# Up projections of two conv-FFN layers by seven block products instead of eight, with the gated hidden rows passed through DRAM

## The chip, the cores and the metric

One core of one Trainium2 chip runs the whole program in one launch. The metric is the device time of that launch in microseconds (us). The kernel before took 2473.97 us (median of 3 runs, 2472.31 to 2477.3).

## The reference, cut to what matters

The program is one inference step of a two-layer decoder trunk for 1024 prompt tokens and 8 requests of 8 tokens, 1088 tokens in all, width 1024. Layer 0 is a recurrent block and a gated conv-FFN; then shared keys and values are projected; layer 1 is sliding-window attention and a second conv-FFN. The change lies in the two conv-FFNs:

```python
D_FF = 3 * D_MODEL          # 3072
def conv_ffn(xn, buf, w_up, conv_w, conv_b, w_down):
    u = xn @ w_up                        # (1088, 1024) @ (1024, 6144)
    g, v = u[..., :D_FF], u[..., D_FF:]
    gc, new_buf = causal_dwconv(g, buf, conv_w, conv_b)   # width 3, along the tokens
    return (jax.nn.gelu(gc) * v) @ w_down, new_buf
```

`xn` is the RMS-normed residual stream. The kernel folds the norm's gain into the input of the product and multiplies by the per-token factor `rstd` behind it.

## The kernel before, in words

Channels lie on the 128 partitions and tokens along the free axis. `x` holds the residual stream as 8 rows (128 channels x 1088 tokens each). Every product keeps fp32 accuracy with three matmuls of a rounded type: an operand is split into a high part (ACT copies it into the rounded type) and a low part (DVE subtracts the high one), and weight-high x data-high, weight-high x data-low and weight-low x data-high are summed in PSUM (lines 886 to 888, function `piece`).

The unit of the order is a weight tile of 1024 x 128: SP loads it into `raw[s]` (slot s is 0 or 1, line 625), ACT makes `whi[s]` (`prep`, line 1426), DVE makes `wlo[s]` (`prep`, line 1977), and PE runs it against the 1088 tokens as three pieces of 384, 384 and 320 tokens, into three of six PSUM banks (slot 0: banks 0 to 2, slot 1: banks 3 to 5). A piece is 8 channel rows x 3 terms = 24 matmuls.

An FFN layer has 24 pairs of up tiles: slot 0 gives 128 channels of g, slot 1 the same channels of v. It goes in 4 blocks of 6 such pairs, and behind each block come 4 pairs of down tiles, which take the block's 6 rows of hidden values from SBUF and add into `x` (`residual`, line 2237). For each up pair DVE rescales g into `convin` (line 2315), runs the width-3 convolution (`conv`, lines 2093 and 2095), ACT takes the GELU (line 1730), DVE multiplies by `rstd` (2337) and by v (2341), and the hidden row is split into `sa` or `sb` (1734, 2348). POOL only copies the convolution's history and new state (2648, 2748, 2749).

Ahead of each FFN stand the 4 pairs of products of the block before it (`N_OUT`, or `N_O` in layer 1). While they run, ACT squares the finished rows of `x` (1649), POOL adds the squares (`add`, 2609), ACT and DVE split the rows (1665, 2263; the last two rows by pieces: 1676, 2274), and PE, ACT and DVE turn the sums into `rstd` (`stats` 916, `root` 1441, `recip` 1994). The split rows wait in SBUF as the input of all 48 up tiles.

The order is written out by hand: each engine has its own in-order program, counting semaphores join them, and the waits stand ahead of the instruction that needs them. SP issues all weight loads in the order of use.

Of the kernel before, what the change touches and what calls it, by code (L numbers as in the profile page):

```python
# [20 lines left out]
P = 128  # L21
# [9 lines left out]
DEC_B = 8  # L31
# [29 lines left out]
N_KV = N_F0 + NFB * (FB + KD // 2)  # L61
# [3 lines left out]
N_END = N_F1 + NFB * (FB + KD // 2)  # L65
# [38 lines left out]
def build(nc, A):  # L104
    with ExitStack() as ctx:
# [23 lines left out]
        reg_end = top[0]  # L129
        raw = [take(f"raw{s}", [P, KD * P], F32) for s in range(2)]  # L130
        whi = [take(f"whi{s}", [P, KD * P], F32R) for s in range(2)]
        wlo = [take(f"wlo{s}", [P, KD * P], F32R) for s in range(2)]
        convin = take("convin", [P, 1120], F32)
        y = take("y", [P, T], F32)
# [64 lines left out]
        def spare(j):  # L199
# [4 lines left out]
                   [spare(11 + k) for k in range(4)] + [spare(j) for j in (1, 3, 5, 15)])  # L204
        fout = at("fout", [18, D_FF], F32, reg_a)
# [48 lines left out]
        hhi_done = sem("hhi_done")  # L254
        hlo_done = sem("hlo_done")
# [63 lines left out]
        x_dram = nc.dram_tensor("x_spill", [P * KD * T], F32, kind="Internal").ap().rearrange("(p k t) -> p k t", p=P, k=KD)  # L319
        strip_in_sb = at("strip_in_sb", [BUCKETS + 1, FV + HEADS], F32, reg_v)  # L320
# [62 lines left out]
        def roots_base(v):  # L383
            return 3 * (v - 1)
# [4 lines left out]
        def xs_tiles(p):  # L389

            return 12 * p
# [196 lines left out]
        def _(eng):  # L588
# [113 lines left out]

            def ffn(layer, n0):
                up, down = A["f_w_up"][layer], A["f_w_down"][layer]
                with eng.Fori(0, NFB) as b:
                    with eng.Fori(0, FB) as j:
                        for s in range(2):
                            load(n0 + b * (FB + KD // 2) + j, s, w_cols(up, s * D_FF + b * (FB * P) + j * P), KD * P)
                    with eng.Fori(0, KD // 2) as i:
                        for s in range(2):  # L710
                            src = down.rearrange("(k p) n -> p k n", p=P)[:, ds(b * FB, FB), ds(i * 256 + s * P, P)]
                            load(n0 + b * (FB + KD // 2) + FB + i, s, src, FB * P)

            ffn(0, N_F0)
# [93 lines left out]
            out_weights(range(2, KD))  # L808
            ffn(1, N_F1)
# [35 lines left out]
        def _(pe):  # L845
# [65 lines left out]
            def stats(v, c):  # L911

                pe.wait_ge(sq_added, sq_base(v) + 22 + c)
                if c == 2:
                    pe.wait_ge(stat_sqrt, roots_base(v) + 1)
                pe.matmul(bank(6 + c % 2, c), ones[:, :], t2[:, chunk(c)], start=True, stop=True).then_inc(stat_ready, 1)  # L916
# [172 lines left out]
            def ffn(layer, n0, m, h, p, v):  # L1089
                hidden_split = ([h[:, k, :] for k in range(FB)], [h[:, FB + k, :] for k in range(FB)])  # L1090

                def block_(b, first, last):
                    nb = n0 + b * (FB + KD // 2)
                    f1 = layer * FT + b * FB + FB
                    if first:
                        unit(nb, 0, KD, m, split_done(p, v))
                        unit(nb, 1, KD, m)
                    with pe.Fori(1 if first else 0, FB) as j:
                        unit(nb + j, 0, KD, m)
                        unit(nb + j, 1, KD, m)  # L1100

                    def hidden(c, k):
                        if c == 0 and k == 0:
                            pe.wait_ge(hlo_done, 3 * f1 - 3)
                        if k == FB - 1:
                            pe.wait_ge(hlo_done, 3 * f1 - 2 + c)
                    if last and layer == 1:
                        for i in range(KD // 2):
                            for s in range(2):
                                pe.wait_ge(hi_ready[s], nb + FB + i + 1)  # L1110
                                pe.wait_ge(lo_ready[s], nb + FB + i + 1)
# [1712 lines left out]
```

## Time and profile before

| | |
|---|---|
| time, median of 3 | 2473.97 us |
| span of the profiled execution | 2473.6 us |
| TensorE (PE) busy | 2461.9 us, 15299 matmuls |
| VectorE (DVE) busy | 1235.0 us |
| ScalarE (ACT) busy | 775.1 us |
| GpSimd (POOL) busy | 270.4 us |
| granted TensorE clock, mean | 0.997 |

The profile is of one execution, whose span is within 0.4 us of the median. PEld is TensorE's loading of weights, which overlaps its matmuls. A matmul's row gives its whole passage, so neighbours overlap; how fast they follow each other is read from their starts. A releaser is what ended an engine's idle time.

### The profile page before, as it was taken

To read this page: it belongs to the slowest core of one execution; us is meant where nothing else is said; L and a number is where in the kernel's file an instruction comes from. 1 tells how busy PE (TensorE), PEld (TensorE's weight loads), DVE (VectorE), ACT (ScalarE), POOL (GpSimd) and SP (SyncE) were. 2 spreads that over 40 slices of the span, in tenths; PEclk is the share of its full clock that TensorE was granted. 3 is DMA by queue.
4 is the path that set the end of the run, shared out by engine and by line. 5 is a ranking of instruction groups with operands and counts; after the bars stand their busy time and mean duration, and the time that the engine had idled before them with its cause. 6 is when DMAs were issued, how large, how long until landed. Compare 5 with 4: busy or idle time off the path is not lost.

```text
span 2473.6 us, 39892 instructions
## 1 busy us (share of the span) xinstructions
PE 2461.9 (100%) x15299; PEld 2407.7 (97%) x15299; DVE 1235.0 (50%) x2008; ACT 775.1 (31%) x1272; POOL 270.4 (11%) x390
## 2 busy tenths in 40 slices
PE   9999999999999999999999999999999999999999
PEld 8999999999999999999999868999999999999999
DVE  7666645434443553444467675455335425434442
ACT  6554633212211321112344684332113113211221
POOL 4212520000000000001220353200000000000000
PEclk9999999999999999999999999999999999999999
DMA  4111111111111111111373203111111111111112
GB/s 127 44 51 43 52 43 43 38 47 51 42 38 47 49 38 49 43 44 37 120 114 72 70 1 107 43 49 40 38 51 42 41 53 42 38 47 51 42 36 92
DMA packets 227190, 130.96 MB, mean 53 GB/s; under 512 B 24789, under 2 KB 224669, under 8 KB 226876
## 3 DMA queue, kind: packets, MB, share of 16 engines
q1 hardware_dynamic: 224948, 126.47, 17.5%
q10 hardware_dynamic: 2100, 3.37, 1.2%
q8 instruction: 53, 0.87, 0.2%
q14 instruction: 25, 0.20, 0.0%
q0 software_dynamic: 64, 0.05, 0.0%
HBM read 116.76 MB, written 15.01 MB: 53 GB/s over the span
## 4 chain that ended last, share of the span: by engine, by line
PE 97%; DVE 1%; ACT 1%; DMA 0%; issue 0%; POOL 0%; POOLq 0%; DVEq 0%; ACTq 0%
PE ps L886 30%; PE ps L888 30%; PE ps L887 30%; PE ps L1264 1%; PE ps L1292 1%; PE ps L1316 1%; PE ps L1187 0%; PE ps L1364 0%; PE ps L1180 0%; PE ps L1365 0%; PE ps L1366 0%; PE ps L1085 0%; PE ps L1066 0%; PE ps L916 0%; PE ps L1198 0%
## 5 line engine op out<-in xcount | busy, mean ns | idle before, releaser
L886 PE MATMUL ps<-sa,whi 128*128 128x384 f32 (+1 forms) x1836 | 600.2, 327 | 0.1
L888 PE MATMUL ps<-sa,wlo 128*128 128x384 f32 (+1 forms) x1836 | 599.1, 326 | 0.0
L887 PE MATMUL ps<-sa,whi 128*128 128x384 f32 (+1 forms) x1836 | 598.6, 326 | 0.0
L886 PE MATMUL ps<-sb,whi 128*128 128x384 f32 (+1 forms) x1764 | 581.8, 330 | 0.0
L888 PE MATMUL ps<-sb,wlo 128*128 128x384 f32 (+1 forms) x1764 | 575.7, 326 | 0.0
L887 PE MATMUL ps<-sb,whi 128*128 128x384 f32 (+1 forms) x1764 | 575.2, 326 | 0.0
L1426 ACT ACTIVATE whi<-raw 128x1024 fp32r<-128x1024 f32 (+1 forms) x201 | 198.3, 986 | 867.1 <-PE ps L888 852.0
L886 PEld LDWEIGHTS ps<-sa,whi 128*128 128x128 f32 x1836 | 344.6, 188 | 1.4 <-issue 0.7
L887 PEld LDWEIGHTS ps<-sa,whi 128*128 128x128 f32 x1836 | 344.6, 188 | 0.3
L888 PEld LDWEIGHTS ps<-sa,wlo 128*128 128x128 f32 x1836 | 344.6, 188 | 0.0
L886 PEld LDWEIGHTS ps<-sb,whi 128*128 128x128 f32 x1764 | 331.3, 188 | 2.8 <-issue 1.2
L887 PEld LDWEIGHTS ps<-sb,whi 128*128 128x128 f32 x1764 | 331.3, 188 | 1.4
L888 PEld LDWEIGHTS ps<-sb,wlo 128*128 128x128 f32 x1764 | 331.1, 188 | 0.0
L1977 DVE TENSOR_TENSOR wlo<-raw,whi 128x1024 fp32r<-128x1024 f32 (+1 forms) x203 | 237.5, 1170 | 149.7 <-ACT whi L1426 149.6
L2237 DVE TENSOR_TENSOR x<-ps,x 128x384 f32 (+3 forms) x216 | 115.0, 534 | 373.8 <-PE ps L888 373.8
L886 PE MATMUL ps<-sc,whi 128*128 128x384 f32 (+1 forms) x816 | 266.8, 327 | 0.2 <-POOL sc L2616 0.2
L888 PE MATMUL ps<-sc,wlo 128*128 128x384 f32 (+1 forms) x816 | 265.9, 326 | 0.0
L887 PE MATMUL ps<-sc,whi 128*128 128x384 f32 (+1 forms) x816 | 265.8, 326 | 0.0
L2315 DVE TENSOR_TENSOR convin<-ps,rstd 128x384 f32<-128x384 f32 x144 | 73.2, 510 | 213.7 <-PE ps L888 212.2
L2748 POOL COPY fstash<-convin 128x2 f32 x48 | 8.9, 184 | 1509.6 <-DVE y L2095 1509.6
L886 PEld LDWEIGHTS ps<-sc,whi 128*128 128x128 f32 x816 | 153.2, 188 | 1.2 <-POOL sc L2616 0.7
L887 PEld LDWEIGHTS ps<-sc,whi 128*128 128x128 f32 x816 | 153.2, 188 | 0.1
(369 smaller groups left out, 2564.1 us busy)
## 6 DMA issues: line engine op xcount, KB each, us to landing
raw<-in_f_w_up SPq DMA_DIRECT2D x96, 512.0 KB, 3.8
raw<-in_f_w_down SPq DMA_DIRECT2D x64, 384.0 KB, 3.4
raw<-in_a_w_in SPq DMA_DIRECT2D x16, 512.0 KB, 3.9
x_spill<-x SPq DMA_DIRECT2D x1, 4352.0 KB, 16.1
x<-x_spill SPq DMA_DIRECT2D x8, 544.0 KB, 5.6
xrows<-in_x_prompt SPq DMA_DIRECT2D x8, 512.0 KB, 7.0
raw<-in_a_w_out SPq DMA_DIRECT2D x8, 512.0 KB, 3.8
raw<-in_w_q SPq DMA_DIRECT2D x16, 256.0 KB, 3.8
```

The source lines that it names most:

```text
L886: pe.matmul(out, whi[s][:, w], mhi[k][:, chunk(c)], start=(k == 0), stop=False)
L887: pe.matmul(out, whi[s][:, w], mlo[k][:, chunk(c)], start=False, stop=False)
L888: last = pe.matmul(out, wlo[s][:, w], mhi[k][:, chunk(c)], start=False, stop=(k == nk - 1))
L1264: last[e] = pe.matmul(out, qz[h0:h0 + HD, 4 * a + j, b * WIN:(b + 1) * WIN], kf[h0:h0 + HD, a, key:key + 256 - k0], start=True, stop=True)
L1292: last = pe.transpose(ps[:, bk, j * P:(j + 1) * P], pb[i % NPB][:, j, h * P:(h + 1) * P], ident[:, :])
L1316: last = pe.matmul(ps[h0:h0 + HD, 6, :], v, pt_buffer(2 * p + e)[h], start=(h == 0 or b == 0), stop=(h == 1))
L1426: act.activation(whi[s][:, 0:cols], raw[s][:, 0:cols], ACT.Copy).then_inc(hi_ready[s], 1)
L1977: dve.tensor_tensor(wlo[s][:, 0:cols], raw[s][:, 0:cols], whi[s][:, 0:cols].bitcast(F32), ALU.subtract)\
L2237: ins = dve.tensor_tensor(xt, bank(b, c), xt, ALU.add)
L2315: dve.tensor_tensor(gp[:, FFN_W - 1 + lo:FFN_W - 1 + lo + w], ps[:, c, 0:w], rstd[:, lo:lo + w], ALU.mult)\
L2748: pool.tensor_copy(fstash[:, ds(f, 1), 0:2], gp[:, SEQ:SEQ + 2].rearrange("p (o w) -> p o w", o=1))
```

## The change

For each of the 24 units (128 channels of g and the same of v), the 1024 input channels are split into even and odd rows, the tokens into two halves of 544, and the outputs into g and v. The 2 x 2 x 2 block product, 8 block products before, is made by 7 with sums and differences of the weight blocks and of the data blocks (Strassen's scheme in Winograd's form). A block product is 4 rows x 3 terms x 2 pieces of 272 tokens = 24 matmuls, 168 in a unit. The seven data blocks (`combos`) are made once in a layer, around the start of its first unit, the sums of the weight blocks in every unit by POOL, and the results are combined from PSUM by ACT, DVE and POOL. All 24 units of a layer now run behind each other and the 16 rounds of down products behind them; a hidden row goes to DRAM when it is made and comes back when its down block needs it. `x` goes to DRAM ahead of the up products, since its place in SBUF is used, and comes back behind them. The down products themselves are as before. In the diff, behind `product` and the entry's `save` and `scale`, stand one unit's order on ACT, one unit's order on DVE, the part of DVE's entry that follows the last residual add, and one unit's order on POOL. A `weight_hi(layer, u, j)` or `weight_lo` is 512 columns of the weight block of product j.

```diff
+HT = T // 2
+HC = HT // 2
...
+        PRODUCTS = [("a", "B11", 0), ("b", "T1", 1), ("c", "B21", 0), ("a", "B22", 1), ("b", "T2", 2), ("c", "T3", 3),
+                    ("d", "T4", 2)]
...
+            def unit_load(layer, u):
+                gu, par = unit_no(layer, u), u % 2
+                if u == 0:
+                    for s in range(2):
+                        eng.wait_ge(lo_ready[s], (N_F0, N_F1)[layer])
+                elif u == 1:
+                    eng.wait_ge(c_lo, combo_at(layer, "T4", "all"))
+                else:
+                    eng.wait_ge(w_lo, NP * (gu - 1))
+                    eng.wait_ge(s_made, 4 * (gu - 1))
+                for s in range(2):
+                    src = w_cols(A["f_w_up"][layer], s * D_FF + u * P).rearrange("p (i e) n -> p i e n", e=2)
+                    for e in range(2):
+                        eng.dma_start(rawu[par][:, s, e, :, :], src[:, :, e, :]).then_inc(unit_raw[par], 16)
...
+            def product(layer, gu, j, before=None):
+                slot, name, g = PRODUCTS[j]
+                pe.wait_ge(w_lo, weights_at(gu, j))
+                if j in (2, 3):
+                    pe.wait_ge(p_copied, 2 * gu + j - 1)
+                elif j == 6:
+                    pe.wait_ge(u2_made, gu + 1)
+                else:
+                    wait(pe, {0: c11_out, 1: c12_made, 4: c21_made, 5: u3_made}[j], gu)
+                hi, lo = SLOT[slot][:, 0, :, :], SLOT[slot][:, 1, :, :]
+                tile = combos[layer][name]
+                more = j in (2, 3)
+                for i in range(4):
+                    for term in range(3):
+                        w = (hi, hi, lo)[term][:, i, :]
+                        for cc in range(2):
+                            if before and term == 0:
+                                before(cc, i)
+                            moving = tile[:, (0, 1, 0)[term], i, cc * HC:(cc + 1) * HC]
+                            last = pe.matmul(ps[:, 2 * g + cc, 0:HC], w, moving, start=(i == 0 and term == 0 and not more),
+                                             stop=(i == 3 and term == 2), skip_group_check=more)
+                last.then_inc(prod, 1)
...
+                def save(k):
+                    act.dma_start(f_dram[:, k, :], x[:, k, :]).then_inc(spilled, 16)
+                def scale(k):
+                    act.wait_ge(spilled, 16 * (KD * layer + k + 1))
+                    act.wait_ge(sq_done, sq_base(v) + 3 * k + 3)
+                    act.activation(x[:, k, :], x[:, k, :], ACT.Copy, scale=pcol[:, k, gain:gain + 1]).then_inc(scaled, 1)
...
+                for u in range(1, FT):
+                    weight_hi(layer, u, 2)
+                    weight_hi(layer, u, 6)
+                    product_copy(layer, u, 0)
+                    weight_hi(layer, u, 3)
+                    gelu(layer, u - 1)
+                    product_copy(layer, u, 1)
+                    weight_hi(layer, u, 4)
+                    weight_hi(layer, u, 5)
...
+                        weight_hi(layer, u + 1, 0)
+                        weight_hi(layer, u + 1, 1)
...
+                for u in range(1, FT):
+                    weight_lo(layer, u, 2)
+                    make_c21(layer, u - 1)
+                    weight_lo(layer, u, 6)
+                    weight_lo(layer, u, 3)
+                    scale_gelu(layer, u - 1)
+                    take_c11(layer, u)
+                    weight_lo(layer, u, 4)
+                    make_hidden(layer, u - 1)
+                    weight_lo(layer, u, 5)
...
+                        weight_lo(layer, u + 1, 0)
+                        make_u2(layer, u)
+                        make_c12(layer, u)
+                        make_u3(layer, u)
+                        weight_lo(layer, u + 1, 1)
+                    unit_conv(layer, u)
...
+                combo_lo(layer, "T2", "all")
+                combo_lo(layer, "T2", 3)
+                weight_lo(layer, 0, 4)
+                recip(v, 0)
+                recip(v, 1)
+                combo_lo(layer, "T3", "all")
+                combo_lo(layer, "T3", 3)
+                weight_lo(layer, 0, 5)
+                seq.settle()
+                take_c11(layer, 0)
+                combo_lo(layer, "T4", "all")
+                combo_lo(layer, "T4", 3)
+                weight_lo(layer, 0, 6)
+                recip(v, 2)
+                make_u2(layer, 0)
...
+                for u in range(1, FT):
+                    unit_state(layer, u - 1)
+                    unit_history(layer, u)
+                    weight_sum(layer, u, 3)
+                    if u < FT - 1:
+                        weight_sum(layer, u + 1, 0)
+                        weight_sum(layer, u + 1, 1)
+                    scale_c12(layer, u)
+                    make_c22(layer, u)
+                    if u < FT - 1:
+                        weight_sum(layer, u + 1, 2)
```

Beside these lines, the change moves the hidden rows: SP's `store(u)` writes a row when `make_hidden` is done, `stage(tt)` reads it back, and ACT's `hidden_hi` and DVE's `hidden_lo` split it, six rows in the last unit and one in each down tile from the second to the seventh of a block; SP's `back(k)` reads row k of `x` back behind the last unit. In the entry, `combo` (POOL, four subtractions of 544 columns for each of four row pairs), `combo_hi` (ACT) and `combo_lo` (DVE) make the split data blocks; the part "all" of a block is its first three rows, 1632 columns.

## Rows read from the trace of the kernel before

**Rows 1.** The page: busy time of the engines, and the chain that ended last.
```profile
PE 2461.9 (100%) x15299; PEld 2407.7 (97%) x15299; DVE 1235.0 (50%) x2008; ACT 775.1 (31%) x1272; POOL 270.4 (11%) x390
...
PE 97%; DVE 1%; ACT 1%; DMA 0%; issue 0%; POOL 0%; POOLq 0%; DVEq 0%; ACTq 0%
```
**Rows 2.** Busy time by engine in one window of up units; clock, DMA share.
```profile
1050.00:1100.00 50.00, 50.00 (x305) 50.00 (x304) 26.66 (x42) 10.54 (x14) 1.03 (x6) 1.00 0.14 42
```
**Rows 3.** Timeline of TensorE, in a piece of 320 and at pieces of 384.
```profile
1000.08 0.31 PE L887 MATMUL ps<-sa,whi 128*128 128x320 f32 x1
...
1001.54 0.31 PE L888 MATMUL ps<-sa,wlo 128*128 128x320 f32 x1
...
1004.84 0.33 PE L886 MATMUL ps<-sc,whi 128*128 128x384 f32 x1
...
1009.00 0.33 PE L886 MATMUL ps<-sc,whi 128*128 128x384 f32 x1
```
**Rows 4.** Instructions grouped by line and form: weight loads, and the cheap vector work.
```profile
L887 PEld LDWEIGHTS ps<-sa,whi 128*128 128x128 f32 x1836 | 344.6, 188 | 0.3
...
L1426 ACT ACTIVATE whi<-raw 128x1024 fp32r<-128x1024 f32 x137 | 144.3, 1053 | 496.8 <-PE ps L888 481.7 <-PE ps L1366 14.9 <-DMA raw<-in_a_w_in 0.2
...
L2337 DVE TENSOR_TENSOR y<-y,rstd 128x1088 f32<-128x1088 f32 x48 | 62.0, 1292 | 56.7 <-ACT y L1730 56.7
...
L1426 ACT ACTIVATE whi<-raw 128x768 fp32r<-128x768 f32 x64 | 54.0, 843 | 370.3 <-PE ps L888 370.3
L1730 ACT ACTIVATE y<-y 128x1088 f32<-128x1088 f32 x48 | 53.5, 1115 | 222.4 <-DVE y L2095 222.4
...
L2237 DVE TENSOR_TENSOR x<-ps,x 128x384 f32 x92 | 51.1, 556 | 149.1 <-PE ps L888 149.1
...
L1994 DVE RECIPROCAL rstd<-rstd 128x384 f32<-128x384 f32 x6 | 15.3, 2550 | 4.7 <-ACT rstd L1441 4.7
```
**Rows 5.** Timeline of DVE: splits of 512 and 1024 columns, and one convolution.
```profile
287.25 0.69 DVE L2250 TENSOR_TENSOR wlo<-raw,whi 128x512 fp32r<-128x512 f32 x1 [0.20 <-ACT whi L1658]
...
374.28 1.23 DVE L1977 TENSOR_TENSOR wlo<-raw,whi 128x1024 fp32r<-128x1024 f32 x1 [0.54 <-ACT whi L1426]
375.43 1.03 DVE L2093 TENSOR_SCALAR y<-convin,fcol 128x1024 f32<-128x1024 f32 x2
376.62 3.10 DVE L2095 SCALAR_TENSOR_TENSOR y<-convin,fcol,y 128x1024 f32<-128x1024 f32 x4 [0.16 <-DVE y L2093]
```
**Rows 6.** Timeline of POOL and DVE: POOL alone (twice), then both at once.
```profile
342.85 1.01 POOL L2609 TENSOR_TENSOR t<-t,t 128x384 f32<-128x384 f32 x1 [4.71 <-ACT t L1649]
...
96.69 2.54 POOL L2730 TENSOR_TENSOR z<-z 128x1088 f32<-128x1088 f32 x1
...
258.31 8.95 POOL L2699 TENSOR_TENSOR sa<-z,sa 128x320 fp32r<-128x320 f32 x6
...
264.74 1.78 DVE L1977 TENSOR_TENSOR wlo<-raw,whi 128x1024 fp32r<-128x1024 f32 x1
```
**Rows 7.** Transposes of 128 columns: six in the timeline; min/median/max ns of one.
```profile
2420.98 0.82 PE L1085 MATMUL ps<-ident,x 128*128 128x128 f32 x6
...
L1085 PE MATMUL ps<-ident,x x72: 270/272/300, 2414.6 to 2469.7; 128*128 128x128 f32 x64, 128*64 128x128 f32 x8
```
**Rows 8.** DMA issues, up weights: KB each and median us from issue to landing.
```profile
raw<-in_f_w_up SPq DMA_DIRECT2D x96, 512.0 KB, 3.8
```
**Rows 9.** Entry of layer 0: last residual add, sum behind the last squares, TensorE's pace.
```profile
361.69 0.48 DVE L2237 TENSOR_TENSOR x<-ps,x 128x320 f32<-128x320 f32 x1
...
353.02 1.01 POOL L2609 TENSOR_TENSOR t<-t,t 128x384 f32<-128x384 f32 x1 [3.35 <-ACT t L1649]
...
361.00:385.00 24.00, 24.00 (x145) 1.00 0.15 45
```
**Rows 10.** Attention: four-matmul groups of 32 columns, then the granted clock by windows.
```profile
1454.98 0.31 PE L1330 MATMUL ps<-pt,cv 128*64 128x32 f32 x4
...
1459.00:1462.00 3.00, 3.00 (x15) 2.24 (x15) 1.02 (x2) 2.24 (x9) 0.00 (x0) 0.50 0.01 3
```

More of the change, by code:

```diff
@@ new lines, in combo_part, with x_half, group, halved @@
+        def combo_part(layer, name, i, part):
+            tile = combos[layer][name]
+            return tile[:, part, 0:3, :] if i == "all" else tile[:, part, i, :]
+        def x_half(k, h):
+            return x[:, k, h * HT:(h + 1) * HT]
+        def group(g):
+            return ps[:, 2 * g:2 * g + 2, 0:HC]
+        def halved(ap):
+            return ap.rearrange("p (c t) -> p c t", c=2)
+        P1S, P5S, U2S, U3S = t1[:, 0:HT], t1[:, HT:T], t2[:, 0:HT], t2[:, HT:T]
+        C12S = y[:, 0:HT]
@@ L1087, in end_job @@
                 last.then_inc(tr_ready, 1)
[L1089 to L1100, printed above, removed]
-                    def hidden(c, k):
[L1103 to L1106, printed above, removed]
+            def product(layer, gu, j, before=None):
[5 more added lines that the diff above has]
+                    pe.wait_ge(u2_made, gu + 1)
+                else:
+                    wait(pe, {0: c11_out, 1: c12_made, 4: c21_made, 5: u3_made}[j], gu)
+                hi, lo = SLOT[slot][:, 0, :, :], SLOT[slot][:, 1, :, :]
+                tile = combos[layer][name]
+                more = j in (2, 3)
[9 more added lines that the diff above has]
+                last.then_inc(prod, 1)
@@ new lines, in ffn, with unit_pair, after_up @@
+            def ffn(layer, n0, v):
+                def unit_pair(h, first=False):
+                    for par in range(2):
+                        if first and par == 0:
+                            first_unit(layer, n0, v)
+                        else:
+                            for j in range(NP):
+                                product(layer, FT * layer + 2 * h + par, j)
+                unit_pair(0, True)
+                with pe.Fori(1, FT // 2 - 1) as h:
+                    unit_pair(h)
+                unit_pair(FT // 2 - 1)
+                for b in range(NFB):
+                    nb, last = n0 + b * (KD // 2), b == NFB - 1
+                    h = hidden_big(layer, b)
+                    hidden_split = ([h[:, k, :] for k in range(FB)], [h[:, FB + k, :] for k in range(FB)])
+                    def hidden(c, k):
+                        if c == 0:
+                            pe.wait_ge(h_lo, FT * layer + FB * b + k + 1)
+                    def after_up(s):
+                        if b == 0:
+                            done = FT * (layer + 1)
+                            for event in ((c11_out, c12_made), (c12_made, c21_made))[s]:
+                                pe.wait_ge(event, done)
@@ L1698, in state_copy @@
+            entry(0, N_OUT, "")
             def state_copy(layer, m):
@@ L1719, in ffn, with down_hi @@
             def ffn(layer, n0, phase):
[L1720 to L1741 removed]
+                def down_hi(s):
+                    act.wait_ge(prod, NP * unit_no(layer, FT - 1) + (4, 6)[s])
+                    prep(n0, s, FB * P, phase)
@@ L1742, in block_ @@
+                gelu(layer, FT - 1)
+                for b in range(NFB):
+                    nd, last = n0 + b * (KD // 2), b == NFB - 1
                     if last and layer == 0:
+                        act.wait_ge(c22_made, FT)
                         with act.Fori(0, KD // 2 - 1) as i:
@@ L2300, in end_copy @@
+            entry(0, N_OUT)
             def end_copy(m):
```

703 lines of the change are left out of this document (541 added, 162 removed).

## The prediction

> **What bounds the kernel now.** I read the page first: TensorE is busy for 2461.9 of 2473.6 us, and the chain that ended last is 97% TensorE [rows 1]. Nothing but its matmuls is worth removing. The windows say the same of the up units alone: 305 matmuls in 50 us, granted clock 1.00, DVE at work for 27 of 50 us, ACT for 11, POOL for 1 [rows 2]. So TensorE is full and the others have room, which is what the change spends. The page's 326 ns of a matmul is its passage, not its pace, so I take the pace from starts in the timeline: ten matmuls of 320 columns from 1000.08 to 1001.54, 146.0 ns each; 24 of 384 columns, the next piece's start included, from 1004.84 to 1009.00, 173.3 ns each [rows 3]. At clock 1.00, the 2.4 GHz level, the columns alone are 133.3 and 160.0 ns: each matmul costs its columns plus 13 ns. An up unit is 144 matmuls, 23.6 us by rows 2, and 48 of them are 1132.8 us.
>
> **The terms.** *Products.* A unit becomes 168 matmuls of 272 columns, 45,696 columns for 52,224: an eighth fewer, but 24 more matmuls. No row has 272 columns. From below, the columns alone are 113.3 ns; from above, the 320-column row, 146.0 ns. The line through the two rows of rows 3 gives 125.5, columns plus 13 ns gives 126.3; I take 126.0. It would fail if loading 128 columns of weights took longer. A load's row says 188 ns [rows 4], but it is a passage too: six transposes, each with its own 128-column load, pass in 0.82 us and one alone in 0.27, so they follow (0.82 - 0.27) / 5 = 0.11 us apart [rows 7]. That is below 126. A unit is then 168 x 0.126 = 21.2 us, 48 are 1016.1: **-116.7 us**.
>
> *Does the vector work keep up?* By columns: a 512-column split is 0.69 us on DVE [rows 5]; on ACT, (1053 - 843) / 256 = 0.82 ns a column gives 0.63 [rows 4]. A 544-column PSUM operation on DVE is 0.72 (556 ns at 384 columns, 1.05 a column from there to the 1292 of 1088 [rows 4]). The convolution is 1.03 + 0.16 + 3.10 = 4.3 [rows 5]. DVE in a unit: 7 x 0.69 + 5 x 0.72 + 4.3 + 2 x 1.29 = 15.3 us of 21.2. ACT: 7 x 0.63 + 2 x 0.6 + 1.1 = 6.8. POOL by rows 6, 1.01 at 384 and 2.54 at 1088 columns, 2.16 ns a column: four weight sums at 1.29, the scaling of the second half of g at 1.3, the fourth output block at 1.36, small copies 0.6: 8.4.
>
> Sums of busy time do not settle it; queues do. The narrowest loop: P5 ends; DVE makes u3 (0.72), splits the next unit's second weights (0.69), convolves (4.3), and only behind that, in its queue, splits the weights of product 2 of the next unit (0.69), for which TensorE waits. With 0.2 from the last matmul's step to its result (passage 0.33 less step 0.17 [rows 3], and a semaphore) that is 6.6 us. TensorE has P6, P0 and P1 to do meanwhile, 72 x 0.126 = 9.1, less 0.2 for the load. In just this stretch POOL makes the fourth block and a weight sum, 2.65 us. Both engines at once slow down: six 320-column subtractions on POOL took 8.95 us where 0.87 each would be 5.2, times 1.7, and DVE's 1024-column split 1.78 [rows 6] for 1.23 [rows 5], times 1.46. So POOL stretches to 4.5 us, DVE loses 4.5 x (1 - 1/1.46) = 1.4, and the loop is 8.0 of 8.9. It holds, by 0.9 us. The next narrowest, the split for product 4 behind `take_c11`, has 1.3 us in hand. The GELU no longer stands between products and down blocks: conv_done comes 1.9 us before ACT reaches it and the copy of P1 is needed 3 us after P1. I take **0** for stalls in the steady units, with 0 and 1.5 us a unit as ends.
>
> The Trainium skill, "GPSIMD Engine Reference", table of specifications, says that GpSimd's SBUF interfaces are shared with VectorE and contend where VectorE has two SBUF inputs. That rule speaks against this change, and rows 6 agree. Were the two fully exclusive, the loop would be 6.6 + 2.65 = 9.25 us of 8.9, 0.35 a unit, some 16 us in all.
>
> *Entry, twice.* Before, it cost nothing: behind the last add at 361.69, 145 matmuls follow in 24 us [rows 9]. Now, with E the end of the last out product:
> - The sum of squares of row 7's first piece is queued on POOL behind ACT, which waits for row 6's copy to DRAM: 4 us by the 512 KB row (3.8) [rows 8]. Before, POOL had it at 353.02 + 1.01, 7.6 us before E [rows 9]; now about 1.3 us after TensorE asks: 1.3.
> - P0 to P3 need only what is early; row 7 comes back scaled at E+7, and P3 ends near E+12.4. P4 needs DVE's part "all" of T2 (1632 columns, 1.9), T2's last row and weights: E+13.8. Then two reciprocals of 2.55 [rows 4] stand in DVE's queue before T3 (1.9 + 0.7) and its weights: P5 starts at E+21.9. P6 needs u2, which is behind c11, T4 (2.6), the weights and a third reciprocal of 320 columns (2.1): E+28.4. Unit 0 ends at E+31.5 instead of 21.2: 10.3.
> - Unit 1's raw weights lie in rows 4 and 5 of `x` and can't be loaded before T4's part "all" is split, E+24. One MB is 2 + 2 x 1.8 = 5.6 us (3.8 for half, of which I take 2 as fixed): E+30. On POOL two weight sums then stand before the scaling that unit 0's convolution needs, so it ends at about E+40, and product 2 of unit 1, due at 37.6, waits 3.1.
> Together 14.7, twice **+29.4 us**. Bounds: 5 (the 1.3 and one gap) and 25 each.
>
> *Clock.* In attention the granted clock fell to 0.50, the 1.2 GHz level, after sixteen groups of four 32-column matmuls, one of which is shown [rows 10]. The entry idles TensorE for 5 and 3.6 us with 3 us of work between. A fall would double P6's 3 us: I take **+6** for both entries; ends 0 and 15.
>
> *End of the up products, twice.* The last unit adds six splits of 1088 columns (1.29) and two of 768 on DVE, 8.4 us net, so 23.7 us for 21.2. But the first down tile asks for rows one at a time; row 5 is split at about +23.3, wanted at 21.2 + 2.6. c21 is ready at 28 to 30, wanted at 30.1. I take **+1** each, ends 0 and 5. Hidden rows (48 of 544 KB out and in) and `x` add some 70 MB to a DMA share of 0.14 [rows 2]; a row is 4 us and waited for in no unit. In the down blocks DVE has 1.65 + 0.96 + 1.29 = 3.9 us of 8.9 per tile (54 matmuls). Price 0; if a row came late, TensorE would wait its 4 us once a block.
>
> Sum: 2473.6 - 116.7 + 29.4 + 6 + 2 = 2394.7, and 0.4 for this execution against the median: **2395 us**.
>
> **The rivals.**
> - *DVE and POOL set the unit* (0.17). The loop above is 1 us longer than worked out, by harder contention or slower semaphores: 0.9 us of slack go, and each further us costs 46. For it: 0.9 us is little. Against: POOL is idle for 60% and the stretch was rated fully overlapped. At 1 us a unit: 2441.
> - *Slower, by weight loading* (0.09). Place: between any two of the 8064 matmuls. If the load can't keep up with 272 columns and the pace stays at the 320-column 146.0 ns, units are 24.5 us, 1177.3 in all: 2473.6 + 44.5 + 37.4 = 2556. It decides from (1132.8 - 37.4) / 8064 = 135.8 ns on. Against: 110 ns in rows 7, although those are plain fp32.
> - *Weights once for two pieces* (0.06). Both pieces now meet the same tile one after the other. The Trainium skill, "TensorE: Matmul & The Clock Gate", step-by-step part, says that weights may be loaded once and used by repeated matmuls. As a mechanism of this kernel: half of the 8064 matmuls would lose the 13 ns, -52 us: 2343. Against: lines 886 and 887 share weights already, and each has a load of its own, 1836 of them at 887 [rows 4], with no shorter step between them.
> - *No eighth less* (0.03): extra stalls of about 2.4 us a unit eat the gain and it comes out even.
>
> **How the numbers follow.** Likeliest (0.65): products at 124 to 129 ns and 15 to 50 us of stalls, 2370 to 2425. The range reaches up into the first rival: 2365 to 2450; outside are the weight-load case, part of the fast one and the worst loop. A measurement of this kernel can tell about 0.2%, 5 us. Faster 0.65 + 0.06 + 0.15 of the first rival = 0.86; within 0.2% 0.03; slower 0.09 + 0.02 = 0.11.
>
> **What would show it.** Starts of 272-column matmuls 126 ns apart; 21.2 us between the same product of two units; TensorE idle in units under 0.3 us; around each entry gaps before T2, T3 and T4 of 1.4, 5 and 3.5 us whose releasers are DVE's splits and u2; the first convolution waiting for POOL's scaling. A DVE release of product 2 in every unit means the first rival; a pace above 136 ns means the second.

## The result, and the profile after

The kernel after took 2395.67 us (median of 4 runs, 2395.09 to 2400.15) against 2473.88 us (4 runs, 2472.31 to 2477.3) for the one before: a ratio of 0.9684, 95% interval 0.967 to 0.9698, 78 us less. The forecast of 2395 us and its sign were right. The profiled execution is the longest of the four, 2400.15 us with a span of 2398.3, so against the span of before, 2473.6, the traces differ by 75.3 us.

The page of the kernel after, busy times and chain; it answers to [rows 1]:

```profile
PE 2350.5 (98%) x16451; PEld 2292.3 (96%) x16451; DVE 1545.9 (64%) x2120; ACT 873.6 (36%) x1486; POOL 823.8 (34%) x758
...
PE 89%; DVE 5%; issue 2%; POOL 1%; DMA 1%; ACT 1%; SPq 0%; POOLq 0%; DVEq 0%; ACTq 0%
```

TensorE has 1152 more matmuls and 111 us less work. DVE has 311 us more and POOL 553 us more; both were meant to be hidden. The chain is still mostly TensorE, but 5% of it is now DVE and 6% others, where it was 97% TensorE. Busy time by engine in two windows of up units (columns as in [rows 2]):

```profile
600.00:650.00 50.00, 50.00 (x402) 50.00 (x401) 39.96 (x49) 16.19 (x25) 25.22 (x25) 1.00 0.22 67
...
1750.00:1800.00 50.00, 50.00 (x401) 50.00 (x400) 38.53 (x48) 15.02 (x23) 26.92 (x25) 1.00 0.33 97
```

TensorE never waits there, at DVE's 40 of 50 us and POOL's 25 to 27. The count of a window takes in matmuls that lie across its edges, so the pace is read from starts. Timeline of TensorE, the last four products of unit 1 (start, duration, tile, shapes, count):

```profile
414.33 3.42 PE L1309 MATMUL ps<-b,slot_a 128*128 128x272 f32 x24
417.59 3.17 PE L1309 MATMUL ps<-t2c,slot_b 128*128 128x272 f32 x24
420.59 3.17 PE L1309 MATMUL ps<-t3c,slot_c 128*128 128x272 f32 x24
423.60 1.66 PE L1309 MATMUL ps<-t4c,slot_d 128*128 128x272 f32 x12
```

From 417.59 to 423.60 are 48 matmuls, 125.2 ns each (126.0 forecast). From unit to unit the same product starts 21.04 or 21.05 us apart in all 44 intervals behind unit 1 of either layer, without one exception. So the steady units have the time that TensorE needs and no more. What is lost lies at their two ends. The waits of TensorE over the whole program (waited for: us in total, times, longest):

```profile
PE ps L1309 <- DVE slot_c L2659: 12.6, 4, 3.5
PE ps L1309 <- DVE slot_b L2659: 6.5, 2, 3.3
PE ps L1309 <- issue: 3.8, 2, 2.0
PE ps L1116 <- POOL t L3078: 3.8, 3, 1.8
PE ps L1309 <- DVE slot_a L2659: 2.0, 2, 1.1
...
PE ps L1083 <- DVE sb L2723: 1.9, 1, 1.9
PE ps L1083 <- DVE sa L2723: 1.9, 1, 1.9
```

Those of up products (L1309) come twice in a layer at most. The timeline of TensorE at layer 0's entry shows where; [rows 9] had 145 matmuls in 24 us here:

```profile
357.74 0.91 PE L1116 MATMUL ps<-t,ones 128*128 128x384 f32 x2 [1.74 <-POOL t L3078]
363.06 3.16 PE L1309 MATMUL ps<-b,slot_a 128*128 128x272 f32 x24
...
374.03 3.17 PE L1309 MATMUL ps<-b,slot_a 128*128 128x272 f32 x24
380.42 4.76 PE L1309 MATMUL ps<-t2c,slot_b 128*128 128x272 f32 x24 [3.22 <-DVE slot_b L2659]
388.03 4.57 PE L1309 MATMUL ps<-t3c,slot_c 128*128 128x272 f32 x24 [2.85 <-DVE slot_c L2659]
394.57 3.23 PE L1309 MATMUL ps<-t4c,slot_d 128*128 128x272 f32 x24 [1.98 <-issue]
398.95 3.27 PE L1309 MATMUL ps<-b,slot_a 128*128 128x272 f32 x24 [1.15 <-DVE slot_a L2659]
...
408.72 5.81 PE L1309 MATMUL ps<-b,slot_c 128*128 128x272 f32 x24 [3.50 <-DVE slot_c L2659]
```

Read the durations too: a product of 24 matmuls passes in 3.17 us, and those behind the long gaps take 4.76, 4.57 and 5.81. There the granted clock has fallen towards the 1.2 GHz level: 0.71 in the window 381 to 389, against 0.98 in 373 to 381. DVE's splits of T2 and T3 in the same stretch, the first with POOL at work and the second with POOL idle:

```profile
374.83 4.72 DVE L2652 TENSOR_TENSOR t2c<-x,t2c 128x1632 fp32r<-128x1632 f32 x2
...
384.95 2.42 DVE L2652 TENSOR_TENSOR t3c<-x,t3c 128x1632 fp32r<-128x1632 f32 x2
```

**Where the 75 us come from.** A unit of the kernel before, 144 matmuls from start to start, in TensorE's timeline:

```profile
1060.99 0.34 PE L886 MATMUL ps<-sb,whi 128*128 128x384 f32 x1
...
1084.71 0.34 PE L886 MATMUL ps<-sb,whi 128*128 128x384 f32 x1
```

Up products: before, 23.72 us a unit (the steps of [rows 3] alone make 96 x 173.3 + 48 x 146.0 ns = 23.64); now 21.05; 48 x 2.67 = 128.2 us less. Entries, by starts: from unit 0's first product (363.06) to unit 1's last (423.60) are 60.54 us, where 13 products of 3.007 and the statistics' matmuls (0.65) would be 39.74; with the gap of 1.74 ahead, 22.5 us. Layer 1: 59.01 and 1.84, 21.1 us. Of these 43.6 us, 29.6 are idle, as the gaps' numbers add up (14.9 and 14.7); 14.0 are matmuls that follow more slowly: stretches at the lower clock, and the refilling of the pipeline behind each gap. Last product to first down tiles: 4.7 and 2.8 us over the matmuls' own time. -128.2 + 43.6 + 7.5 = -77.1, where the spans differ by 75.3. Of the 1.8 us between them 1.3 lie in attention, which the change does not touch: from its first to its last product of queries and keys are 95.5 us in this execution of the kernel before and 96.8 in this one of the kernel after. In the other traces that stretch is 94.0 to 96.8 us, so it is scatter.

### The profile page after: what moved, and what is told of

The parts are those of the page before. It is cut to its first block, busy times and chain, and to the rows that moved or that the text cites. A ratio compares the mean times of both kernels' runs of the same rounds, so it can differ in the third digit from the quotient of the medians.

```text
span 2398.3 us, 41262 instructions
## 1 busy us (share of the span) xinstructions
PE 2350.5 (98%) x16451; PEld 2292.3 (96%) x16451; DVE 1545.9 (64%) x2120; ACT 873.6 (36%) x1486; POOL 823.8 (34%) x758
## 4 chain that ended last, share of the span: by engine, by line
PE 89%; DVE 5%; issue 2%; POOL 1%; DMA 1%; ACT 1%; SPq 0%; POOLq 0%; DVEq 0%; ACTq 0%
PE ps L1309 38%; PE ps L1083 15%; PE ps L1085 14%; PE ps L1084 14%; PE ps L1520 1%; PE ps L1548 1%; PE ps L1572 1%; DVE y L2458 0%; PE ps L1443 0%; DMA stage<-h_spill 0%; DMA rawu<-in_f_w_up 0%; POOL t L3078 0%; DVE rstd L2359 0%; PE ps L1620 0%; PE ps L1436 0%
## 5 line engine op out<-in xcount | busy, mean ns | idle before, releaser
L1083 PE MATMUL ps<-sa,whi 128*128 128x384 f32 (+1 forms) x972 | 318.9, 328 | 2.4 <-DVE sa L2723 1.9
L1085 PE MATMUL ps<-sa,wlo 128*128 128x384 f32 (+1 forms) x972 | 317.6, 327 | 0.0
L1084 PE MATMUL ps<-sa,whi 128*128 128x384 f32 (+1 forms) x972 | 317.3, 326 | 0.0
L1309 PE MATMUL ps<-b,slot_a 128*128 128x272 f32 x2304 | 304.6, 288 | 2.0 <-DVE slot_a L2659 2.0
L1083 PE MATMUL ps<-sb,whi 128*128 128x384 f32 (+1 forms) x900 | 300.7, 334 | 2.6 <-DVE sb L2723 1.9
L1309 PEld LDWEIGHTS ps<-b,slot_a 128*128 128x128 f32 x2304 | 295.3, 189 | 2.5 <-DVE slot_a L2659 2.5
L1085 PE MATMUL ps<-sb,wlo 128*128 128x384 f32 (+1 forms) x900 | 294.7, 327 | 0.0
L1084 PE MATMUL ps<-sb,whi 128*128 128x384 f32 (+1 forms) x900 | 294.4, 327 | 0.0
L1083 PEld LDWEIGHTS ps<-sa,whi 128*128 128x128 f32 x972 | 182.8, 188 | 3.9 <-DVE sa L2723 2.2
L1084 PEld LDWEIGHTS ps<-sa,whi 128*128 128x128 f32 x972 | 182.8, 188 | 0.1
L3078 POOL TENSOR_TENSOR t<-t,t 128x384 f32<-128x384 f32 (+1 forms) x72 | 73.0, 1024 | 319.7 <-ACT t L1905 297.4
L1085 PEld LDWEIGHTS ps<-sa,wlo 128*128 128x128 f32 x972 | 182.7, 188 | 0.0
L1083 PEld LDWEIGHTS ps<-sb,whi 128*128 128x128 f32 x900 | 169.7, 189 | 5.7 <-DVE sb L2723 2.2
L1084 PEld LDWEIGHTS ps<-sb,whi 128*128 128x128 f32 x900 | 169.6, 188 | 1.1
L1085 PEld LDWEIGHTS ps<-sb,wlo 128*128 128x128 f32 x900 | 169.5, 188 | 0.0
L1309 PE MATMUL ps<-b,slot_c 128*128 128x272 f32 x1152 | 157.3, 294 | 8.1 <-DVE slot_c L2659 7.0
L1309 PE MATMUL ps<-t2c,slot_b 128*128 128x272 f32 x1152 | 155.3, 292 | 6.5 <-DVE slot_b L2659 6.5
L1309 PE MATMUL ps<-t3c,slot_c 128*128 128x272 f32 x1152 | 155.0, 291 | 5.6 <-DVE slot_c L2659 5.6
L1309 PEld LDWEIGHTS ps<-b,slot_c 128*128 128x128 f32 x1152 | 151.5, 193 | 9.2 <-DVE slot_c L2659 7.4
```

The lines of the kernel that those rows point to most:

```text
L1083: pe.matmul(out, whi[s][:, w], mhi[k][:, chunk(c)], start=(k == 0), stop=False)
L1084: pe.matmul(out, whi[s][:, w], mlo[k][:, chunk(c)], start=False, stop=False)
L1085: last = pe.matmul(out, wlo[s][:, w], mhi[k][:, chunk(c)], start=False, stop=(k == nk - 1))
L1309: last = pe.matmul(ps[:, 2 * g + cc, 0:HC], w, moving, start=(i == 0 and term == 0 and not more), stop=(i == 3 and term == 2), skip_group_ ...
L3078: pool.tensor_tensor(t2[:, chunk(c)], t2[:, chunk(c)], t1[:, chunk(c)], ALU.add).then_inc(sq_added, 1)
```

## Experiments

Ten kernels ran, each an edit of the kernel after. Times are medians (`widths` ran once), ratios are against the kernel before on the same chip; the kernel after is at 0.9684, and an interval reaches 3.5 to 5.6 us to either side, so where the times can't decide the traces do. A trace is one execution too: in the four kernels whose edits don't touch the entry (`dum1`, `dum2`, `nopool`, `sp`) the stretch of 60.54 us above is 58.9 to 59.8 us, and layer 1's of 59.01 is 58.7 to 59.1.

**1. How near is the steady loop to setting the unit?** On DVE, one operation more (544 columns, 0.71 us where POOL is idle) in units from the third on, ahead of the convolution (`dum1`), or two (`dum2`). That is 22 units a layer, 44 in all, and not the 46 of the expectations:

```diff
+                for _ in range(1 if u > 1 else 0):      # dum2: 2
+                    seq.mark(dve.tensor_tensor(U2S, U2S, U2S, ALU.max))
+                    seq.settle()
                 conv(FFN_W, 2, ...)
```

> One operation more on VectorE in each unit from the third on (a maximum over 128x512, about 0.69 us by the split of the same size), ahead of the two conversions; 46 units have it. Theory A (the loop from the third sum to the split of the next unit's product 2 takes about 8.15 us of the 8.9 us that it has, so 0.75 us are free): 0 to 0.3 us a unit, 0 to +12 us in all, at most a few stalls at product 2. Rival (VectorE and POOL set the unit's time): +0.7 us a unit, +31 us. Rival (there is much more room than the loop suggests): no change, within 2 us.

> Two such operations more in each of 46 units, 1.4 us. Theory A (0.75 us free): 0.65 us a unit, more where the clock falls with the stall: +30 to +50 us, with a wait for product 2's term in each unit. Rival (VectorE and POOL set the unit already): +1.4 us a unit, +64 us. Rival (more room than the loop suggests): under +5 us.

Measured: 2405.24 us (0.9719, 0.9703 to 0.9735) and 2438.68 us (0.9858, 0.9842 to 0.9874), +9.6 and +43.0. Timeline of TensorE with two operations more:

```profile
608.55 3.27 PE L1309 MATMUL ps<-b,slot_c 128*128 128x272 f32 x24 [0.70 <-DVE slot_c L2659]
...
630.56 3.26 PE L1309 MATMUL ps<-b,slot_c 128*128 128x272 f32 x24 [0.70 <-DVE slot_c L2659]
```

A unit is 22.01 us, 0.96 more, and product 2 waits for its weights in each; by starts the units behind unit 1 take 20.8 and 20.2 us more in the two layers, 41 of the 43.0 us. With one operation a unit is 21.14 us, 0.09 more, and 4.1 us in all. The loop from u3 (line 2687) to the split for product 2 is 0.75 us longer with one operation and 1.63 with two. So the first 0.66 us are free, not the 0.9 of the forecast, and what comes on top is paid in full. The rival that DVE and POOL set the unit already would have cost 31 us for the first operation; it falls, by little. The +9.6 of `dum1` is more than its 4.1 us; the trace has 2.9 us more at the end of the up products (last product to the first 320-column down matmul, 14.34 and 14.62 us for 13.96 and 12.04), where the last unit has the operation too. The rest is within the intervals.

**2. Why is the loop as long as it is?** Timeline of DVE in the kernel after, the loop in question, and of POOL beside it; then the convolution's first pass by single operations (duration in ns, min/median/max):

```profile
865.78 0.72 DVE L2687 TENSOR_TENSOR t<-ps,t 128x544 f32<-128x544 f32 x1 [1.52 <-PE ps L1309]
866.42 0.68 DVE L2659 TENSOR_TENSOR slot_b<-wsum,slot_b 128x512 fp32r<-128x512 f32 x1
867.02 3.05 DVE L2458 TENSOR_SCALAR y<-convin,fcol 128x1024 f32<-128x1024 f32 x2
870.10 3.00 DVE L2460 SCALAR_TENSOR_TENSOR y<-convin,fcol,y 128x1024 f32<-128x1024 f32 x4
873.02 0.68 DVE L2659 TENSOR_TENSOR slot_c<-rawu,slot_c 128x512 fp32r<-128x512 f32 x1
```

```profile
866.59 1.73 POOL L3279 TENSOR_TENSOR x<-t,t 128x544 f32<-128x544 f32 x1 [0.75 <-DVE t L2687]
868.27 1.74 POOL L3228 TENSOR_TENSOR wsum<-rawu,wsum 128x512 f32<-128x512 f32 x1
```

```profile
L2458 DVE TENSOR_SCALAR y<-convin,fcol x2: 1282/1564/1845, 867.0 to 868.8; 128x1024 f32<-128x1024 f32 x1, 128x64 f32<-128x64 f32 x1
```

The first pass, 1.03 us in [rows 5], is 3.05 here. It runs exactly beside POOL's two sums, and its second operation, 64 columns only, starts at 868.8, takes 1.28 us and ends 0.06 us after POOL's sum. The experiment `nopool` takes POOL's work away from there:

```diff
-                pool.tensor_tensor(hidden_row(u % 2)[:, HT:T], U3S, P5S, ALU.add).then_inc(c22_made, 1)
+                n_ = 16 if u > 1 else HT
+                pool.tensor_tensor(hidden_row(u % 2)[:, HT:HT + n_], U3S[:, 0:n_], P5S[:, 0:n_], ALU.add).then_inc(c22_made, 1)
```

and the weight sum in line 3228 makes only 4 of 128 columns of each row. What is left of the two sums is 16 of 544 columns and 4 x 4 of 4 x 128; the rest is left out, so the kernel serves for its times alone.

> Left out of each unit from the third on: most of GpSimd's last quadrant sum of the hidden rows and of its weight combination of the token-independent kind (4 of 272 and of 544 columns or so are still made), so the hidden rows and one weight combination are not the full ones; TensorE's and VectorE's work stay as they are. Theory A (VectorE's pair of 3.05 us ahead of the split, 1.03 us alone, is long because GpSimd works beside it, and the loop has 0.75 us to spare): the pair's member falls to about 1.0 us, the loop gets some 2 us shorter, the pace of the matmuls is 125 ns as before, and the time is the same within 2 us. Rival (the loop sets the unit): the unit gets shorter, -10 us or more. Rival (the pair is long for another reason): the pair stays at 3.05 us.

Timeline of DVE in this kernel:

```profile
696.82 0.72 DVE L2687 TENSOR_TENSOR t<-ps,t 128x544 f32<-128x544 f32 x1 [1.52 <-PE ps L1309]
697.46 0.68 DVE L2659 TENSOR_TENSOR slot_b<-wsum,slot_b 128x512 fp32r<-128x512 f32 x1
698.06 1.03 DVE L2458 TENSOR_SCALAR y<-convin,fcol 128x1024 f32<-128x1024 f32 x2
699.12 3.00 DVE L2460 SCALAR_TENSOR_TENSOR y<-convin,fcol,y 128x1024 f32<-128x1024 f32 x4
702.04 0.68 DVE L2659 TENSOR_TENSOR slot_c<-rawu,slot_c 128x512 fp32r<-128x512 f32 x1
```

The pass is 1.03 us again, to the digit, and the loop 5.90 us instead of 7.92: POOL's work, which takes 2.65 us alone (1.36 and 1.29), costs DVE 2.02 us. What is left of it here, 0.60 and 0.66 us in the same place, costs DVE nothing that shows. The time was 2388.53 us (0.9656, 0.9641 to 0.9672), 7.1 less, where I had expected it the same within 2. The loop does not explain that: units are 21.00 us, 0.05 less, 2.1 in all. The rest is at the end of the up products, where the last product to the first 320-column down matmul takes 10.21 and 10.27 us instead of 13.96 and 12.04: 5.5 us. There the last unit's splits stand behind this loop, and it had no slack: TensorE's wait for DVE's split of the hidden rows is 0.7 us in either layer instead of 1.9.

`dum2` says something of the mechanism:

```profile
622.12 3.61 DVE L2704 TENSOR_TENSOR t<-t 128x544 f32<-128x544 f32 x2
625.76 1.03 DVE L2458 TENSOR_SCALAR y<-convin,fcol 128x1024 f32<-128x1024 f32 x2
```

Whatever stands beside POOL's sums pays, here the two added operations (1.42 us alone, 3.61), and the convolution behind them is untouched. The loss is 2.0 to 2.2 us either way: it belongs to the stretch, not to the kind of DVE operation. The Trainium skill, "SBUF — State Buffer", section "SBUF: two separate sides", says that the port pair shared by VectorE and GpSimd is locked for a whole instruction, for a VectorE instruction in a two-port mode or, against one of GpSimd that reads SBUF, one with two SBUF inputs, and that the other engine stands still. The 64-column operation that ended 0.06 us after POOL's is what such a lock looks like, and so is the order of the four ends (POOL 868.32, DVE 868.87, POOL 870.01, DVE 870.07), as if the engines took turns. POOL waits too (1.73 and 1.74 us for 1.36 and 1.29), so the 2.02 us that DVE loses for 2.65 us of work do not speak against it. No run tests the lock by itself.

**3. Does the order of the two pieces matter?** In `ccout` a weight tile isn't met by both pieces in turn:

```diff
-                for i in range(4):
-                    for term in range(3):
-                        w = (hi, hi, lo)[term][:, i, :]
-                        for cc in range(2):
+                for cc in range(2):
+                    for i in range(4):
+                        for term in range(3):
+                            w = (hi, hi, lo)[term][:, i, :]
```

> The loop over the two 272-token pieces is put outside the loops over tile rows and terms, so that a weight tile is no longer met by both pieces in turn; the number of matmuls and of weight loads stays. Theory A (each matmul loads its weights anyway, and the order of the pieces is worth nothing): pace 124.6 ns as in the changed kernel, same time within 2 us. Rival (a weight tile that is met twice in turn is loaded once or cheaper): the pace goes to about 131 ns, +2.1 us for each of 48 units in part, up to +52 us.

Measured: 2398.63 us (0.9695, 0.9679 to 0.9712), every unit 21.04 or 21.05 us. Meeting a tile twice in turn is worth nothing here; that rival is out.

**4. What does a matmul cost by its width?** `widths` cuts the pieces of four products, and is read for its pace alone:

```diff
+        PARTS = [(272,), (136, 136), (208, 64), (240, 32), (176, 96), (272,), (272,)]
...
+                            for wd in PARTS[j]:
+                                moving = tile[:, (0, 1, 0)[term], i, cc * HC + at_:cc * HC + at_ + wd]
```

> The moving pieces of the seven products have other widths: product 0, 5 and 6 keep 2 pieces of 272, product 1 has 4 of 136, product 2 208 and 64, product 3 240 and 32, product 4 176 and 96 tokens in each half. One look, for the price of one matmul by width. Theory A (a matmul takes its columns at 2.4 GHz and some 11 ns more, but never less than its weight load): 124.6 ns at 272, about 110 ns at 136, 96, 64 and 32, 111 to 113 ns at 240 and 110 at 208 and 176. Rival (the fixed part is paid by every matmul and there is no floor): 68 ns at 136, 38 ns at 64. Rival (the floor lies at 120 ns and sets the pace at 272 too): 120 ns or more at every width. The whole gets longer by 24 matmuls more in four products of 48 units: some 4,600 at 110 ns less what the narrower pieces save, about +400 us.

Timeline of TensorE in this kernel:

```profile
621.39 5.49 PE L1312 MATMUL ps<-b,slot_c 128*128 128x208 f32 x48
626.72 5.52 PE L1312 MATMUL ps<-b,slot_a 128*128 128x240 f32 x48
632.09 5.54 PE L1312 MATMUL ps<-t2c,slot_b 128*128 128x176 f32 x48
637.47 3.24 PE L1312 MATMUL ps<-t3c,slot_c 128*128 128x272 f32 x24
...
643.55 3.17 PE L1312 MATMUL ps<-b,slot_a 128*128 128x272 f32 x24
646.56 5.47 PE L1312 MATMUL ps<-t1c,slot_b 128*128 128x136 f32 x48
651.87 3.44 PE L1312 MATMUL ps<-b,slot_c 128*128 128x208 f32 x29
```

(A row is named by the first width of its product.) By starts: 136 columns 110.6 ns each; 208 and 64 together 2 x 111.0; 240 and 32 2 x 111.9; 176 and 96 2 x 112.1; 272 125.4. Within a pair the starts are uneven (180 and 43 ns for 208 and 64), so only the means count: whatever the two widths below 272, a matmul costs 110 to 112 ns in the mean. There is a floor, and 272 columns are above it. The forecast's 0.11 us between loads [rows 7] held for the rounded type too. The floor is not a price of every instruction. In the kernel before, the second group of matmuls behind the one of [rows 10], of 32 columns with loads of 64:

```profile
1455.45 0.31 PE L1330 MATMUL ps<-pt,cv 128*64 128x32 f32 x4
```

From 1454.98 eight matmuls take 0.47 us, 59 ns each; they start in pairs, 118 ns for two loads of 64 columns. That is in keeping with a floor that goes by the columns loaded. No run changes the load of the up products alone: that their floor is the load fits, but is not shown by itself. The time was 2830.15 us, 434 more. The Trainium skill, "TensorE: Matmul & The Clock Gate", section "LDWEIGHTS (loading the stationary operand)", gives a load as its columns over 1.2 GHz, 107 ns for 128; the floor of 110.6 ns agrees.

**5. What is late in the entry?** `late` moves the reciprocals of unit 0 behind the splits of T3 and T4 in DVE's program, and with them `take_c11`, while `make_u2` comes ahead of the reciprocals, and unit 1's first two weights ahead of the third reciprocal and of u3; `late_lo2` also moves product 2's weights of unit 1 ahead of the first convolution:

```diff
                 weight_lo(layer, 0, 4)
-                recip(v, 0)
-                recip(v, 1)
                 combo_lo(layer, "T3", "all")
...
                 weight_lo(layer, 0, 6)
+                make_u2(layer, 0)
+                recip(v, 0)
+                recip(v, 1)
...
                 make_u3(layer, 0)
+                weight_lo(layer, 1, 2)                  # late_lo2
                 unit_conv(layer, 0)
```

> At the entry of the up products only VectorE's order changes: the reciprocals of unit 0 go behind the token sums t3 and t4 and their splits. Theory A (what comes late in the changed kernel's entry is what VectorE does ahead of each sum): the gap of 2.85 us ahead of product 5 is gone or under 0.5 us, the one of 1.98 us ahead of product 6 falls to 0 to 0.6 us, unit 1 starts about E+31 us instead of E+35.9 us, where E is the first up product; but product 2 of unit 1 now waits for its term behind the reciprocals, some 5 us instead of 3.5. In all 3 us less per entry, -6 us for the two (-3 to -8). Theory B (the entry is set by the arrival of unit 1's raw weights, which the trace shows waited for): product 5 starts earlier and unit 1 starts no earlier than E+35 us, and the time is the same within 1 us.

> As the run before it, and the low part of unit 1's weights for product 2 is moved ahead of the two conversions of unit 0 (3.0 us each) on VectorE. Theory A (VectorE's order decides the entry): the stall of 3.50 us at product 2 of unit 1 is gone too; product 3 of that unit may now stall up to 3.5 us, since its term is queued behind the conversions. The entry gains 4 to 6 us, -8 to -12 us for the two layers if product 3 does not stall, -6 if it does. Theory B (raw weights set it): as with the run before it, same within 1 us, and the wait is only moved.

Measured: 2391.06 us (0.966, 0.9644 to 0.9676) and 2386.16 us (0.9642, 0.9626 to 0.9658), 4.6 and 9.5 less. Timeline of TensorE in `late_lo2`:

```profile
363.24 3.16 PE L1309 MATMUL ps<-b,slot_a 128*128 128x272 f32 x24
...
380.60 4.77 PE L1309 MATMUL ps<-t2c,slot_b 128*128 128x272 f32 x24 [3.23 <-DVE slot_b L2659]
385.21 3.17 PE L1309 MATMUL ps<-t3c,slot_c 128*128 128x272 f32 x24
388.22 3.17 PE L1309 MATMUL ps<-t4c,slot_d 128*128 128x272 f32 x24
393.49 3.27 PE L1309 MATMUL ps<-b,slot_a 128*128 128x272 f32 x24 [2.11 <-DVE slot_a L2659]
...
406.66 5.81 PE L1309 MATMUL ps<-b,slot_a 128*128 128x272 f32 x24 [3.48 <-DVE slot_a L2659]
```

Products 5 and 6 follow product 4 without a gap, and unit 1 starts at E+30.25 instead of E+35.9, where theory B had it no earlier than E+35. From the first product to unit 1's last the two layers take 55.11 and 55.61 us instead of 60.54 and 59.01: 8.8 us less, or some 7.5 against the four kernels with an untouched entry. With `late` alone 56.33 and 57.8, and product 2 of unit 1 waits for 4.76 us, as expected. With the weights ahead of the convolution that wait is gone and product 3 has one of 3.48: the wait moved on by one product, but it shortened what came before. So DVE's order decides, but theory B has a part in it. Timeline of ACT in `late`, layer 1, unit 1's first weights:

```profile
1594.40 0.63 ACT L1967 ACTIVATE slot_a<-rawu 128x512 fp32r<-128x512 f32 x1 [7.04 <-DMA rawu<-in_f_w_up]
```

TensorE waits 3.30 us for them there. The load does hold unit 1; it starts behind the split of T4, and moving the reciprocals brought that split, and so the load, forward.

**6. The last gap ahead, and the end of the up products.** `sq` puts row 7's first sum and square ahead of row 6's scaling; `sp` issues the fourth down stage ahead of the last store:

```diff
+                    if u == FT - 1:
+                        stage(3)
...
-                for tt in range(3, FB):
+                for tt in range(4, FB):
```

> At the end of the attention block, the sum and the square of the last row's first column tile are made ahead of the preceding row's scaling, on VectorE and ScalarE. Theory A (the statistics of the last row are the one gap ahead of the first up product, 1.74 us, and they are late by what stands ahead of them on these two engines): the gap shrinks to 0.2 us or less, -1.5 us per layer, -3 us in all. Theory B (POOL's share of the statistics sets it, the releaser that the trace names): the gap stays at 1.7 us, same time within 1 us.

> On SyncE's queue the load of the fourth stage for the down projection is issued ahead of the last store of the gated rows instead of behind it. Theory A (the down stage starts late because a load stands behind a store that waits for the last conversion): the gaps of 0.72 and 1.90 us after the last up product and the half clock that follows them shrink, 2 to 4 us per layer, -4 to -8 us in all. Theory B (VectorE's conversions of the last unit and its splits for the down stage set it): both gaps stay where they are and the time is the same within 1 us.

Measured: `sq` 2394.56 us (0.9669, 0.9647 to 0.9692), `sp` 2392.85 us (0.9674, 0.9657 to 0.969). Neither can be told from the kernel after by its time. The traces can. In `sq` the statistics' matmuls wait in neither layer:

```profile
356.55 0.91 PE L1116 MATMUL ps<-t,ones 128*128 128x384 f32 x2
```

In `sp` the gap of 0.72 us and the slow matmuls behind the second gap (0.52 us of passage for 0.33) are gone, but that gap, for a DVE split, stays at 1.79 and 1.23 us; last product to first 320-column matmul is 11.34 and 10.78 us for 13.96 and 12.04, 3.9 us less. In the traces of the kernels that leave this end alone (`ccout`, `late`, `late_lo2`, `sq`) it is 12.9 to 13.9 and 11.8 to 13.4, so the gain is clear of their scatter.

**7. All of it together**, `best`: the edits of `late_lo2`, `sq` and `sp`.

> The three edits in one kernel with the whole computation: the last row's statistics first, the fourth stage's load ahead of the last store, the reciprocals behind the splits of the entry and unit 1's low part ahead of the conversions. If the gains add: about 2386 us as in the run with the entry's order alone, less 1 to 3 us for the statistics and 2 to 4 us for the stage, 2380 to 2383 us. Rival (the entry is bound by the same chain whichever gap is taken away, so a gap closed ahead opens one later): 2385 to 2387 us.

Measured: 2378.22 us (median of 5, 2374.21 to 2383.56; 0.961, 0.9594 to 0.9626), 17.5 us less than the kernel after and 96 less than the one before. The gains add, within the intervals: the single medians had given 9.5 + 1.1 + 2.8 = 13.4. The profiled executions place 14.7 of their 18.3 us (entries 6.5 and 2.3, statistics 3.6, last product to down tiles 2.3; layer 0's part of it, 12.91 us, is no shorter than in the kernels without the edit). The other 3.6 lie in the layers' middle, 2.8 of them in attention, where the kernel after has a granted clock of 0.93 in two windows of 50 us and this one 0.97; no edit touches that, and `ccout` and `sp` have 0.97 too, so I count it as scatter. What stays in layer 0's entry are, above all, gaps of 3.22, 0.90 and 3.47 us.

## Why the prediction was right

- **Products**: 126.0 ns forecast, 125.2 measured; 21.2 us a unit, 21.05 measured. The saving was 128.2 us for 116.7; of the 11.5 between them half are this pace and half the 23.6 us of before, read off a window's count, where starts give 23.72. Columns plus 13 ns held from 384 to 272 columns, within 1 ns; at 136 it would give 70 ns, and 110.6 were measured.
- **No stalls in steady units**: right, for a worse reason than stated. POOL's contention was put at 1.4 us from a ratio of [rows 6] and is 2.02; other terms were a little long (the loop measures 7.92 us for 8.0). The slack was 0.66 rather than 0.9. The rated factor hid that a 64-column operation can wait a microsecond for the engine beside it.
- **Entry**: idle 29.6 us for 29.4, the right sum with parts that were off. Product 4 came at E+17.4, not 13.8. Row 7 was scaled at E+8, not 7, and DVE's split of T2, priced at 2.6 us with its last row, took 4.72 beside a weight sum and a block sum on POOL (1.77 and 2.95 us from 374.30 on), which the step left out; the same splits of T3 and T4, with POOL idle, took 2.42 and 2.48. Ahead of it two 544-column splits took 3.10 beside two more block sums. Everything behind slid by 3 to 4 us (25.0, 31.5 and 35.9 for 21.9, 28.4 and 31.5), so the gaps ahead of T3 and T4 came out smaller, 2.85 and 1.98 us for 5 and 3.6. Again the mis-sized term is POOL beside DVE. Behind it the chain of raw weights, weight sums and scaling held as forecast: the first convolution starts at 402.06, right behind POOL's scaling (401.96), and product 2 of unit 1 waits 3.50 us for 3.1.
- **Clock**: mis-sized, +6 for 14 us (with refilling). The fall was foreseen for one product an entry; it slowed parts of three, behind the gaps of 3.22, 2.85 and 3.50 us.
- **End of the up products**: +1 each forecast, 4.7 and 2.8 us measured. The step looked at DVE's load alone. SP's queue was part of it: the load of the fourth stage stood behind a store that waits for the last but one hidden row.
- **Sum**: against the profiled execution -75.3 measured, -79.3 forecast (-116.7 + 37.4; the text on record adds up to 2394.3, not 2394.7, a slip of 0.4). Products were 11.5 us better, the overhead (51.1 for 37.4) 13.7 worse, and 1.8 us lie outside both, most of it in attention. That the median of 2395.67 lies within 1 us of the forecast is a meeting of these errors with a profiled execution 4.5 us above its median.
- **Rivals**: narrow matmuls have a floor, at 110.6 ns, under the 135.8 from which weight loading would have decided. Weights once for two pieces: no difference in either order. DVE and POOL as the bound: not at this load, and at 1.4 us more a unit they are. No eighth less: it took 2.4 us of stalls a unit, and 51.1 us over 48 units are 1.1.

## What to carry to other kernels

When a change trades TensorE work for vector work, write out the narrowest queue loop of the slower engines and price the stretch where POOL and DVE read SBUF together at most of POOL's own time, however short DVE's operations are. Then look at the ends: a pipeline that is free when it runs here lost 51 of 128 us in two fillings and two drainings, and it was the order of the engines' programs in them, DVE's above all, and not any amount of work, that some 14 to 17 us hung on. A shorter matmul pays only down to a floor: measure it, here 110 ns, before cutting tiles narrower.

## What the runs showed of the hardware

- DVE's 64-column tensor_scalar took 1.28 us beside a POOL sum, and its pair with one of 1024 columns (1.85 us there) is 1.03 us where POOL has next to nothing to do. The loss moved to whatever DVE did in the stretch.
- With the same 128x128 weights loaded for each, matmuls of 136 columns, and pairs of 64 and 208, 32 and 240 or 96 and 176, follow every 110 to 112 ns in the mean, of 272 columns every 125.
- In `nopool` a product of 24 matmuls took 3.00 us instead of 3.007 and a unit 21.00 instead of 21.05, in all 44 intervals. Matmuls of 320 and 384 columns keep their pace. The step of 3.00 us is there already in unit 1 (414.62 to 423.62), ahead of the first shortened sum at 426.32, so it is not the missing work of POOL as such. I did not find why.
